# Down products of a PEER channel mixer: token weights stationary, 512 table columns moving, and a turn back at each layer's end

## What is computed

```python
def peer_ffn(h, w_q, k1, k2, u_tab, v_tab):
    ...
        ug = u_tab[ic]
        act = jax.nn.gelu(jnp.einsum('td,thkd->thk', xc, ug), approximate=False)
        vg = v_tab[ic]
        return jnp.einsum('thk,thkd->td', gc * act, vg)
    ...
for i in range(DEPTH):
    ...
    x = x + g2[:, None, :] * peer_ffn(h, peer_w_q[i], peer_k1[i], peer_k2[i], peer_u[i], peer_v[i])
return rmsnorm(x, final_g)
```

## Time and profile before

| | |
|---|---|
| median of 3 runs | 1956.16 us (1953.42 to 1958.62) |
| profiled execution: its own time | 1951.68 us |
| its span, first to last instruction | 1949.9 us |
| mean granted clock | 0.989 |
| TensorE, VectorE, ScalarE busy | 97%, 79%, 44% |

### The profile page before, as it was taken

How to read it: one execution, slowest core, us unless ns; L and a number is a source line. 1 busy time by engine, 2 the same in 40 slices (tenths; PEclk the granted TensorE clock), 3 DMA queues, 4 the chain that set the end, 5 groups by cost and what they waited for, 6 DMA issues and landing times.

```text
span 1949.9 us, 46087 instructions
## 1 busy us (share of the span) xinstructions
PE 1898.2 (97%) x17828; PEld 1886.7 (97%) x17828; DVE 1539.2 (79%) x2886; ACT 857.0 (44%) x1277; POOL 4.0 (0%) x8
## 2 busy tenths in 40 slices
PE   5989999999999999999999999999999999999998
PEld 5989999999999999999999899999999999999998
DVE  7986688878888888778778669888788888875554
ACT  3335444444334444444444544445433444444443
POOL 0000000000000000000000000000000000000000
PEclk9999999999999999999989999999999999999999
DMA  8985455545444444688845645555544444455552
GB/s 305 331 299 205 147 183 184 180 159 168 156 151 157 156 162 162 252 300 299 299 135 174 245 151 184 182 183 171 163 153 152 151 162 162 160 184 174 182 183 97
DMA packets 101343, 370.43 MB, mean 190 GB/s; under 512 B 11168, under 2 KB 11552, under 8 KB 100640
## 3 DMA queue, kind: packets, MB, share of 16 engines
q1 hardware_dynamic: 100848, 367.43, 54.9%
q10 hardware_dynamic: 432, 2.23, 0.3%
HBM read 366.47 MB, written 3.15 MB: 190 GB/s over the span
## 4 chain that ended last, share of the span: by engine, by line
PE 90%; DVE 7%; DMA 1%; issue 1%; ACT 1%; SPq 0%; DVEq 0%; ACTq 0%
PE ps L1065 45%; PE acc L1065 38%; PE gp L1163 5%; DVE low L542 2%; DVE acts L561 2%; PE gp L1025 1%; PE gp L1152 1%; DMA acts<-w_mod 0%; PE gp L1036 0%; DVE acts L614 0%; ACT high L361 0%; DMA raw<-conv_out 0%; DVE acts L906 0%; DMA raw<-conv_in 0%; PE gp L1052 0%
## 5 line engine op out<-in xcount | busy, mean ns | idle before, releaser
L542 DVE TENSOR_TENSOR low<-raw,high 128x1024 fp32r<-128x1024 f32 x596 | 727.0, 1221 | 356.8 <-ACT high L361 351.8
L361 ACT ACTIVATE high<-raw 128x1024 fp32r<-128x1024 f32 x593 | 626.0, 1056 | 534.9 <-PE acc L1065 427.3
L1065 PE MATMUL ps<-mov_h,high 128*128 128x256 f32 x2704 | 780.7, 289 | 17.7 <-DVE mov_l L620 7.2
L1065 PE MATMUL ps<-mov_l,high 128*128 128x256 f32 x2704 | 769.8, 285 | 0.0
L1065 PE MATMUL ps<-mov_h,low 128*128 128x256 f32 x2704 | 769.4, 285 | 0.0
L1065 PE MATMUL acc<-mov_h,high 128*128 128x256 f32 x2048 | 585.1, 286 | 1.4 <-DVE mov_l L965 1.4
L1065 PE MATMUL acc<-mov_l,high 128*128 128x256 f32 x2048 | 579.1, 283 | 0.0
L1065 PE MATMUL acc<-mov_h,low 128*128 128x256 f32 x2048 | 579.0, 283 | 0.0
L1065 PEld LDWEIGHTS ps<-mov_h,high 128*128 128x128 f32 x2704 | 523.0, 193 | 21.5 <-issue 17.9
L1065 PEld LDWEIGHTS ps<-mov_l,high 128*128 128x128 f32 x2704 | 524.0, 194 | 0.0
L1065 PEld LDWEIGHTS ps<-mov_h,low 128*128 128x128 f32 x2704 | 523.6, 194 | 0.0
(11 more groups left out here) (101 smaller groups left out, 724.6 us busy)
## 6 DMA issues: line engine op xcount, KB each, us to landing
raw<-up SPq DMA_DIRECT2D x256, 512.0 KB, 3.3
raw<-down SPq DMA_DIRECT2D x256, 512.0 KB, 3.3
acts<-w_mod SPq DMA_DIRECT2D x84, 512.0 KB, 4.8
raw<-query SPq DMA_DIRECT2D x32, 512.0 KB, 3.4
raw<-conv_in SPq DMA_DIRECT2D x24, 512.0 KB, 6.6
acts<-w_mod SPq DMA_DIRECT2D x6, 1024.0 KB, 14.7
raw<-conv_out SPq DMA_DIRECT2D x8, 512.0 KB, 7.4
raw<-pool_in SPq DMA_DIRECT2D x8, 512.0 KB, 3.3
```

The lines of the kernel that those rows point to most:

```text
L361: nc.scalar.activation(flat(high[s]), tile_row(s), ACT.Copy).then_inc(high_ready, 1)
L542: nc.vector.tensor_tensor(flat(low[n % RING]), tile_row(n % RING), flat(high[n % RING]).bitcast(F32), ALU.subtract).then_inc(low_ready, 1)
L1065: ins = nc.tensor.matmul(dst, w[s][:, c], m[:, mv], start=(first and n == 0), stop=(last and n == 2), skip_group_check=skip)
```

## The change

In `down_tile` the operands trade places. The 128 token weights of a half of the tokens become the stationary operand (`mov_h` or `mov_l`), and 512 columns of `high` or `low` move. A tile is then 4 banks x 3 = 12 matmuls of 512 columns. Bank `b` holds tokens `b % 2` on the partitions and channel half `b // 2` along the free dimension, so `acc` now lies the other way round from `X`. At each layer's end ScalarE copies banks 0 and 2 and VectorE banks 1 and 3 to a new buffer `E` in `acts` (its place belongs to token weights that have been used by then), TensorE turns `E` back by 16 float32 matmuls of 128 columns against the identity (into `ps` for the first four chunks, into banks 0 and 1 of `acc` for the last four), and the residual reads that.

```diff
+        E = part(B0, TC * D).rearrange("p (tc n) -> p tc n", tc=TC)
...
+        def turned_back(c):
+
+            b = (ps, acc)[c // 4]
+            return b[:, c % 4 // 2, (c % 2) * T:(c % 2 + 1) * T]
...
+                for b in (0, 2):
+                    act.wait_ge(acc_done, 3 * layer + b + 1)
+                    nc.scalar.activation(E[:, b % 2, (b // 2) * 512:(b // 2 + 1) * 512], acc[:, b, :], ACT.Copy
+                                         ).then_inc(acc_out_act, 1)
             norm(4)
...
+                for b in (1, 3):
+                    if b == 1:
+                        dve.wait_ge(acc_done, 3 * layer + 2)
+                    else:
+                        dve.wait_ge(product, n0 + KEYS + RING)
+                    nc.vector.tensor_copy(E[:, b % 2, (b // 2) * 512:(b // 2 + 1) * 512], acc[:, b, :]
+                                          ).then_inc(acc_out_dve, 1)
                 dve.wait_ge(reloaded, 16 * (layer + 1))
                 for c in range(DC):
-
-                    if c % 2 == 0 and c < DC - 2:
-                        dve.wait_ge(acc_done, 3 * layer + c // 2 + 1)
-                    elif c % 2 == 0:
-                        dve.wait_ge(product, n0 + KEYS + RING)
-                    nc.vector.scalar_tensor_tensor(X[:, c], acc[:, c // 2, (c % 2) * T:(c % 2 + 1) * T],
+                    if c % 2 == 0:
+                        dve.wait_ge(back, (layer * DC + c) // 2 + 1)
+                    nc.vector.scalar_tensor_tensor(X[:, c], turned_back(c),
...
-                        for c in range(DC):
-                            ins = three(acc[:, c // 2, (c % 2) * T:(c % 2 + 1) * T], s, c, s, False, closing, True)
-                            if closing and c % 2 and c < DC - 1:
+                        for b in range(4):
+                            tok = slice(b % 2 * P, (b % 2 + 1) * P)
+                            cols = slice(b // 2 * 512, (b // 2 + 1) * 512)
+                            for n, (v, w) in enumerate(((high, mov_h), (low, mov_h), (high, mov_l))):
+                                ins = nc.tensor.matmul(acc[:, b, :], w[:, s, tok], flat(v[s])[:, cols], start=False,
+                                                       stop=(closing and n == 2), skip_group_check=True)
+                            if closing and b < 3:
                                 ins.then_inc(acc_done, 1)
...
+                for c in range(DC):
+                    if c % 4 == 0:
+                        pe.wait_ge(acc_out_act, 2 * layer + c // 4 + 1)
+                        pe.wait_ge(acc_out_dve, 2 * layer + c // 4 + 1)
+                    for tc in range(TC):
+                        ins = nc.tensor.matmul(turned_back(c)[:, tc * P:(tc + 1) * P], E[:, tc, c * P:(c + 1) * P],
+                                               eye, start=True, stop=True)
+                    if c % 2:
+                        ins.then_inc(back, 1)
```

More of the change, by code:

```diff
@@ L218, in program @@
         acc_done = sem("acc_done")
+        acc_out_act = sem("acc_out_act")
+        acc_out_dve = sem("acc_out_dve")
+        back = sem("back")
         step = sem("step")
```

## The result

The changed kernel takes 1923.83 us (median of 4 runs, 1923.22 to 1925.29) against 1956.62 us before (median of 4). The ratio is 0.9836, 95% interval 0.9824 to 0.9848: faster by 33 us, or 1.6%. Forecast were 1884 us and a range of 1871 to 1921, so the direction held, the gain came out at less than half, and the time lies 3 us above the range. The profiled execution took 1923.58 us, its span is 1921.8.

What follows compares the result with a forecast made beforehand. TensorE's solid stream of down products was taken as the bound: 74.7 us gained there less 3.7 us at the layers' ends is 71.0 us, giving a forecast of 1884 us, range 1871 to 1921.

Steps and rivals of the forecast that it cites:

- Where the limit is: Whole kernel: TensorE, busy 97% of the span, bounds it; its down products are a solid stream.
- The covers: Down stage: VectorE and DMA keep up with the shorter tiles, VectorE with 0.5 us to spare per first-half pair.
- the price of one wide matmul: Down products: 512 columns take 216.0 ns, between 213.3 and 218; 3072 of them gain 74.7 us.
- the warm row: Layer 1's second half, clock 1.00: 256-column matmuls start 120.2 ns apart, 13.5 ns more than their columns.
- The low-clock row: Same 256-column matmuls at clock 0.50: starts 0.215 us apart against 213.3 ns of columns, so nothing is added.
- The residue of 2.7 ns: Wide down products: a small rest above 213.3 ns of columns, taken from other rows, giving 216.0 ns.
- a fixed price per matmul: Rival for the down products: the whole 13.5 ns stays, 226.8 ns per matmul, 1918 us; chance 0.10.
- the layers' ends: Ends of both layers with the turn back: +2.1 us in layer 1, +1.5 in layer 0, 3.7 taken.
- columns at the warm rate: Rival for the down products: 240.3 ns per 512 columns, nothing gained, 1960 us; chance 0.05.
- bare loads: Rival for the down products: weight loads wait for the columns' end, 326 ns per matmul, 2224 us; chance 0.02.
- overlapping products: Rival for the down products: they take much less than their columns, VectorE sets the pace, 1762 us; chance 0.01.
- VectorE did not take over: Rival in the down stage: contention makes VectorE the bound, half the gain goes, 1921 us; chance 0.03.

Runs made afterwards that it cites:

- e5_noturn: Changed kernel without the copies to E and the 16 turning matmuls, the residual reading acc as it lies: 1918.05 us, ratio 0.9805.
- e8_dense: Changed kernel with down products reading only constant dense bf16, moving 512, 128, 256 and 64 columns by stretch: 1904.64 us in one run.
- the transposing kernel: Changed kernel with the 16 turning matmuls in TensorE's transpose mode, one pass over float32 instead of two: 1921.47 us, ratio 0.9818.

## Why the prediction was wrong, step by step

- **Where the limit is: right.** TensorE's stream of down products was the bound and stayed it. The covers held: TensorE waits 1.7 us in all of the down products, VectorE idles 0.7 us in a pair of tiles of a first half, and the DMA carried the shorter second half of layer 0 (310 GB/s at a share of 0.85, TensorE busy all of the time).
- **The step that failed: the price of one wide matmul.** "The nearest row is the one at the low clock: what decides whether the load is hidden is the 213 ns that it has to hide in". One measured 227.1 ns, not 216.0: 3072 x 11.1 = 34 us of the 43 by which the 28.1 us between the spans fall short of the 71.0 forecast. The 13.5 ns of the warm row were not an uncovered end of the load, which 213 ns would have covered, but a price of each matmul at the high clock, 13.5 for 256 columns and 13.8 for 512 at 128 stationary ones; the sums with 384 and 320 columns leave 14.7 and 12.4. The low-clock row was read rightly and still holds for 512: three starts of the last tile, two intervals, are 0.85 us apart, and 512 / 1.2 is 427 ns. What was wrong is to carry its zero over to the high clock.

```profile
987.00 0.63 PE L1231 MATMUL acc<-high,mov_h 128*128 128x512 f32 x1
987.43 0.63 PE L1231 MATMUL acc<-low,mov_h 128*128 128x512 f32 x1
987.85 0.63 PE L1231 MATMUL acc<-high,mov_l 128*128 128x512 f32 x1
```

- **The residue of 2.7 ns** that I took from bf16 and two-pass rows is real, for dense bf16: 2.5. The two-pass float32 rows, 111 ns apart, were no sign of it: 112 ns is what a stream goes by when it waits for loads of 128 four-byte columns. The rows that carried the 13.5 were the very type and layout of the new products, and all of them were warm. They were nearer than either.
- **The rival "a fixed price per matmul" is what happened.** It had 0.10, and 226.8 ns against 227.1. Its 1918 us fell short by 6, and its gain of 37.9 us (41.6 - 3.7) is 9.8 above the 28.1 between the spans. Most of that is three terms: the layers' ends, whose 3.7 us it took over, 2.9 too little; the slower last tile (1.6); and the dearer first halves (2.8). The range then ended 3 us above that one value, although the case's own uncertain terms (ends up to 6 us, base up to 1958.6) would have carried it to 1923, still a little short of 1923.8; its weight deserved more, its width too.
- **The layers' ends: mis-sized, 3.7 against 6.6 us.** The failing words are "its four square sums 0.4". Only the last chunk's sums were counted behind the last square, as if the others had been made during the turn. In the chain they stand in one line: 16 turning matmuls (3.57 us), then 32 records of square sums (3.48 us), 7.06 us together. Without the turn (e5_noturn) the end is back at 3.48.
- **Not in the sum at all:** the lower clock for the last tile of layer 0 (1.6 us) and the dearer hand-over to the scatter (2.8 us), which the forecast took over as 0.80 us per pair.
- **The other rivals:** columns at the warm rate (240 ns), bare loads (326 ns) and overlapping products are each excluded by 227.1; VectorE did not take over.

## What to carry to other kernels

Price a matmul by rows of its own type and layout, and split the distance of starts into columns over clock and a rest; if no row shows the rest at another width, a fixed rest is the first guess, not the last. Twice the width then halves that rest per column (13.6 ns of 120 here), no more. What is put on an engine behind its stream is added to what already stands there in order: count the whole queue, not the last link of the chain.

## What the runs showed that was not expected

- A matmul whose moving columns lie four bytes apart takes about 13.6 ns more than its columns at the clock of 1.00, the same for 256 (120.2 ns) and 512 (227.1 ns), and nothing more at 0.50; with dense bf16 columns it is 2.5 (109 and 216 ns). It holds for bf16 read from every second place too (11.9 to 13.6 ns, at 512 columns), with still operands and in both orders of banks tried, and falls to some 9.6 ns with 96 stationary columns instead of 128. That reading the moving columns and loading the next weights get in each other's way would fit this; it was not shown.
- The load of 4-byte weights has its own pace in the stream, 112 ns for 128 columns and 85 for 96, so by estimate fp32r matmuls of fewer than some 236 moving columns ((112 - 13.6) x 2.4) go by the load; the pairs with 192 and 128 columns fit this, and no width between 192 and 256 was run. Dense bf16 has no such limit down to 64 columns: each of the matmuls 29.4 ns apart in e8_dense has a load of 128 columns of its own, of always the same weights.
- In layer 0's end the granted clock falls from 1.00 to 0.50 during or soon after a run of matmuls with one moving column, in every kernel traced, though TensorE is busy just ahead of the fall (from 1910 to 1912 in the transposing kernel it falls so in layer 1 too, mean 0.53 at 2.00 us busy of 2.00). Taking work out ahead of them can move the fall to a dearer place.
